# Block of two layers at one core: the first layer's projections, compressions and loads in another order

## What is computed

```python
def nsa_pool_mixer(x, w_in, cmp_pos, cmp_w1, cmp_b1, cmp_w2, pool_w, pool_scale, w_out):
    h = x @ w_in                       # columns: q 512 | six k/v of 128 | 24 gates | pool input u 512
    q = ...; kv = ...; gates = jax.nn.sigmoid(h[..., o2:o3]); u = h[..., o3:]
    k_cmp, v_cmp, k_slc, v_slc, k_win, v_win = kv
    kc = compress_blocks(k_cmp, cmp_pos[0], cmp_w1[0], cmp_b1[0], cmp_w2[0])   # gelu(blocks @ w1 + b1) @ w2
    vc = compress_blocks(v_cmp, cmp_pos[1], cmp_w1[1], cmp_b1[1], cmp_w2[1])
    ...                                # softmax over 15 compressed blocks -> o_c,
    ...                                # over the selected blocks -> o_s, over the window -> o_w
    o = gb[..., 0:1] * o_c + gb[..., 1:2] * o_s + gb[..., 2:3] * o_w
    o_pool = pool_mixer(u, pool_w, pool_scale)
    return jnp.concatenate([o_nsa, o_pool], axis=-1) @ w_out
```

## Time and profile before

| | |
|---|---|
| median of the runs | 1427.62 us |
| profiled execution | 1425.51 us, of it 1423.8 us span |
| PE (matmul) | 1313.5 us busy, 92% |
| PE weight loads | 1226.6 us, beside the matmuls |
| DVE | 832.3 us, 58% |
| ACT | 598.6 us, 42% |
| POOL | 176.6 us, 12% |
| chain that ended last | PE 77%, DVE 7%, ACT 6%, DMA 5%, POOL 3% |
| mean granted clock of PE | 0.953 |

### The profile page before, as it was taken

How to read it: one execution, slowest core, us unless ns; L and a number is a source line. 1 busy time by engine, 2 the same in 40 slices (tenths; PEclk the granted TensorE clock), 3 DMA queues, 4 the chain that set the end, 5 groups by cost and what they waited for, 6 DMA issues and landing times.

```text
span 1423.8 us, 20987 instructions
## 1 busy us (share of the span) xinstructions
PE 1313.5 (92%) x9100; PEld 1226.6 (86%) x9100; DVE 832.3 (58%) x970; ACT 598.6 (42%) x694; POOL 176.6 (12%) x136
## 2 busy tenths in 40 slices
PE   4898889999899879999898999889989899999996
PEld 4887789999799679999798999789989799999995
DVE  4425685555752785555769537764467665555554
ACT  3225544334464343433466237533743443333331
POOL 7030040000400040000221300031120300000002
PEclk9868999999999999999899999999999899999999
DMA  7350255555451545656689335963455436555550
GB/s 228 89 148 1 89 179 192 192 182 197 125 179 59 177 141 188 200 182 164 111 109 164 64 72 80 154 92 65 142 164 190 136 130 211 192 178 180 193 191 30
DMA packets 155021, 205.03 MB, mean 144 GB/s; under 512 B 9395, under 2 KB 137122, under 8 KB 154930
## 3 DMA queue, kind: packets, MB, share of 16 engines
q1 hardware_dynamic: 152706, 195.80, 49.6%
q0 software_dynamic: 2224, 7.90, 1.6%
HBM read 202.63 MB, written 1.05 MB: 143 GB/s over the span
## 4 chain that ended last, share of the span: by engine, by line
PE 77%; DVE 7%; ACT 6%; DMA 5%; POOL 3%; issue 2%; POOLq 0%; SPq 0%; DVEq 0%; ACTq 0%
PE PS L353 22%; PE PS L354 21%; PE PS L355 21%; DMA ring<-in_w_in 4%; DVE w_lo L965 2%; ACT w_hi L1514 2%; PE PS L810 2%; PE PS L822 1%; PE PS L818 1%; POOL lvl L1867 1%; POOL AR L1954 1%; ACT AR L1544 1%; DMA ring<-in_a_w_out 1%; PE PS L588 1%; DVE AR L1291 1%
## 5 line engine op out<-in xcount | busy, mean ns | idle before, releaser
L965 DVE TENSOR_TENSOR w_lo<-ring,w_hi 128x2048 fp32r<-128x2048 f32 x183 | 436.2, 2389 | 277.5 <-ACT w_hi L1514 267.4
L353 PE MATMUL PS<-x_hi,w_hi 128*128 128x256 f32 x1696 | 499.0, 294 | 37.4 <-DVE x_lo L1009 13.5
L354 PE MATMUL PS<-x_lo,w_hi 128*128 128x256 f32 x1696 | 490.6, 289 | 0.0
L355 PE MATMUL PS<-x_hi,w_lo 128*128 128x256 f32 x1696 | 489.9, 289 | 0.0
L1514 ACT ACTIVATE w_hi<-ring 128x2048 fp32r<-128x2048 f32 x183 | 349.2, 1911 | 314.7 <-PE PS L355 262.6
L353 PEld LDWEIGHTS PS<-x_hi,w_hi 128*128 128x128 f32 x1696 | 337.3, 199 | 45.1 <-DVE w_lo L965 24.9
L354 PEld LDWEIGHTS PS<-x_lo,w_hi 128*128 128x128 f32 x1696 | 337.0, 199 | 3.6 <-issue 2.0
L355 PEld LDWEIGHTS PS<-x_hi,w_lo 128*128 128x128 f32 x1696 | 336.3, 198 | 0.0
L1526 ACT ACTIVATE AR<-PS 128x512 f32<-128x512 f32 (+2 forms) x148 | 84.4, 584 | 332.8 <-PE PS L355 218.0
L353 PE MATMUL PS<-w_hi,o_hi 128*128 128x512 f32 x480 | 188.5, 393 | 4.2 <-DVE o_lo L1162 4.2
L354 PE MATMUL PS<-w_lo,o_hi 128*128 128x512 f32 x480 | 187.4, 390 | 0.0
(11 more groups left out here) (358 smaller groups left out, 1413.5 us busy)
## 6 DMA issues: line engine op xcount, KB each, us to landing
ring<-in_mlp_w SPq DMA_DIRECT2D x64, 1024.0 KB, 5.3
ring<-in_w_in SPq DMA_DIRECT2D x32, 1024.0 KB, 10.4
ring<-in_expert_w_gate SPq DMA_DIRECT2D x16, 1024.0 KB, 5.4
ring<-in_expert_w_up SPq DMA_DIRECT2D x16, 1024.0 KB, 5.4
ring<-in_expert_w_down SPq DMA_DIRECT2D x16, 1024.0 KB, 4.9
ring<-in_c_w_in SPq DMA_DIRECT2D x12, 1024.0 KB, 5.4
ring<-in_a_w_in SPq DMA_DIRECT2D x7, 1024.0 KB, 8.6
ring<-in_c_w_out SPq DMA_DIRECT2D x4, 1024.0 KB, 5.0
```

The lines of the kernel that those rows point to most:

```text
L353: mm(out, a_hi, b_hi, start=first, stop=False, skip_group_check=True)
L354: mm(out, a_hi, b_lo, start=False, stop=False, skip_group_check=True)
L355: return mm(out, a_lo, b_hi, start=False, stop=last, skip_group_check=True)
L965: v.tensor_tensor(w_lo[:, m % PARTS], ring[:, index[split[m]] % RING], w_hi[:, m % PARTS].bitcast(F32), ALU.subtract)\
```

## The change

- x is loaded in two halves, the first weight chunk too, and both are split half by half (ACT and DVE: x's two first pairs, first half of the weights, x's other pairs, second half). DVE no longer splits two whole chunks before x's low part; PE starts aq 0 when the first half is split.
- Chunks: aq 0, acmp, aq 1, au 0, au 1, cmp_w1, "ak" (both keys), "av" (both values). So acmp comes second, au before the keys, and keys and values fill a chunk each: ak is one `by_feature`, av one `by_token`, 48 matmuls of 256 columns each.
- ac1 is 16 matmuls of 60 columns with 128-column stationaries (both compressions side by side, loaded as two DMAs), and one stands after each of the 16 triples of au 1.
- The gates: 24 matmuls of 256 columns with the weights stationary, then two transposes of the result ("agT").
- Scores against compressed keys: 8 matmuls of 30 columns for 16 of 15. They stand before av, so that av's matmuls run while the compressed softmax is made.
- DVE's reciprocal covers 64 elements; the counts need fewer POOL instructions and come before POOL's level masks.
- The vector loads (16) follow three weight chunks; the small loads are in three groups between later chunks. The narrow weights are split in two parts.
- DVE's and ACT's splits of the first two output chunks stand elsewhere: on ACT both before the reading of av; on DVE one before the first maxima, one after the third.

The core of the diff (the loads and the split of the head; cut at "..."):

```diff
-        cols("aq", aw, 0, 2)
+        cols("aq", aw, 0, 1)
         cols("acmp", aw, 512, 1)
-        cols("akv", aw, 768, 2)
-        chunks.append(("cmp_w1", [((0, P), A["a_cmp_w1"][0].rearrange("v (k p) n -> p v k n", p=P), (2 * 16, 64))]))
+        cols("aq", aw, 256, 1, 1)
         cols("au", aw, 1304, 2)
+        chunks.append(("cmp_w1", [(v, A["a_cmp_w1"][0, v].rearrange("(k p) n -> p k n", p=P), (16, 64)) for v in range(2)]))
+        for name, c in (("ak", 768), ("av", 768 + P)):
+            chunks.append((name, [(a, aw[:, c + W * a:c + W * a + P].rearrange("(k p) n -> p k n", p=P), (KT, P)) for a in range(2)]))
...
+            by_feature(("aq", 0), lo=4, ready=[("xT", j) for j in range(4)], halves="first_lo")
             x_ready(-1)
-            by_feature(("aq", 1))
             by_feature(("acmp", 0))
...
+            by_feature(("aq", 1))
+            by_feature(("au", 0))
+            steps = triples(("au", 1), nxt())
             arrived(pe, "cmp_w1")
...
-            for v in range(2):
-                for k in range(16):
-                    ins = mm(ps[0:64, v * 32:v * 32 + 30], w[:, v, k, :], a_kb[:, v, k].rearrange("p g c -> p (g c)"), start=(k == 0), stop=(k == 15))
+            for k in range(16):
+                advance(steps, 1)
+                ins = mm(ps[:, 0:60], w[:, k, :], a_kb[:, :, k].rearrange("p v g c -> p v (g c)"), start=(k == 0), stop=(k == 15))
             close(ins, "ac1")
...
+            ins = with_x(ps[:, 0:T], "wga")
+            close(ins, "ag")
...
+            by_feature("ak")
...
+                    ins = mm(ps[:, o:o + 30], a_q[:, i, t * P:(t + 1) * P], a_kc.rearrange("p g c -> p (g c)"), start=True, stop=True)
+            close(ins, "asc")
+            by_token("av")
...
+            for h in range(2):
+                for j in (2 * h, 2 * h + 1):
+                    ve.wait_ge(S("x0_hi"), j + 1)
+                    ps = full(ve, ("xT", j))
+                    evacuated(v.tensor_tensor(flat(x_lo[:, 2 * j:2 * j + 2]), ps, flat(x_hi[:, 2 * j:2 * j + 2]).bitcast(F32), ALU.subtract), ("xT", j))
+                half = slice(h * PIECE // 2, (h + 1) * PIECE // 2)
+                ve.wait_ge(S("hi_split" if h else "first_hi"), 1)
+                ins = v.tensor_tensor(w_lo[:, 0, half], ring[:, 0, half], w_hi[:, 0, half].bitcast(F32), ALU.subtract)
...
-            v.reciprocal(a_rc, a_rc).then_inc(S("win_recip"), 1)
+            v.reciprocal(a_rc[:, :, 0:16], a_rc[:, :, 0:16]).then_inc(S("win_recip"), 1)
...
+                if n == 2:
+                    split_ahead(pieces_for["av"])
...
             for n, (name, parts) in enumerate(chunks):
-                if n == 2:
+                if n == RING:
                     load_vectors()
```

More of the change, by code:

```diff
@@ L355, in products, with by_feature @@
                 return mm(out, a_lo, b_hi, start=False, stop=last, skip_group_check=True)
-            def by_feature(chunk, a_hi=x_hi, a_lo=x_lo, lo=0, hi=8, ready=None, layer=None):
-                n = take(chunk)
+            def by_feature(chunk, a_hi=x_hi, a_lo=x_lo, lo=0, hi=8, ready=None, layer=None, halves=None):
+                if halves is not None:
+                    pe.wait_ge(S(halves), 1)
+                    n, reached[0] = part[chunk] % PARTS, part[chunk] + 1
+                else:
+                    n = take(chunk)
                 wh, wl = colview(w_hi, n), colview(w_lo, n)
@@ L366, in by_feature @@
                             read_out(pe, ready[k // 2])
+                        if m == 0 and k == 4 and halves is not None:
+                            take(chunk)
                         if m == 0 and k % 4 == 0 and layer is not None:
@@ L1560, in layer_norm, with queries @@
                     high_half(l, 1, 0)
-            for j in range(4):
-                ps = bank(("xT", j))
-                a(flat(x_hi[:, 2 * j:2 * j + 2]), ps, ACT.Copy).then_inc(S("x0_hi"), 1)
-            for j in range(2):
-                ps = bank(("aq", j)).rearrange("p (m t) -> p m t", m=2)
+            for h in range(2):
+                for j in (2 * h, 2 * h + 1):
+                    ps = full(act, ("xT", j))
+                    a(flat(x_hi[:, 2 * j:2 * j + 2]), ps, ACT.Copy).then_inc(S("x0_hi"), 1)
+                half = slice(h * PIECE // 2, (h + 1) * PIECE // 2)
+                if h:
+                    arrived(act, split[0])
+                else:
+                    act.wait_ge(S("first_weights"), 16)
+                a(w_hi[:, 0, half], ring[:, 0, half], ACT.Copy).then_inc(S("hi_split" if h else "first_hi"), 1)
+            pieces[0] = 1
+            def queries(j, ahead):
+                ps = bank(("aq", j), ahead).rearrange("p (m t) -> p m t", m=2)
                 for half in range(2):
@@ L1580, in _, with pool_input @@
-            act.wait_ge(S("small"), SMALL)
-            a(n_hi[:], narrow, ACT.Copy).then_inc(S("narrow_hi"), 1)
-            copy("ag", a_g, lambda ps: ps[:, 0:TT * 24].rearrange("p (t n) -> p t n", t=TT), func=ACT.Sigmoid)
-            ps = bank("ac1")
+            def pool_input(j):
+                ps = bank(("au", j), 1)
+                evacuated(a(a_u[0][:, 2 * j:2 * j + 2, 16:16 + T], ps.rearrange("p (a b) -> p a b", a=2), ACT.Copy), ("au", j))
+            queries(0, 2)
+            split_ahead(pieces_for[("acmp", 0)])
@@ L1590, in _ @@
             evacuated(ins, "ac1")
-            for j in range(2):
-                copy(("au", j), a_u[0][:, 2 * j:2 * j + 2, 16:16 + T], lambda ps: ps.rearrange("p (a b) -> p a b", a=2))
+            pool_input(1)
+            act.wait_ge(S("small"), SMALL)
+            a(n_hi[:, NARROW_PARTS[1]], narrow[:, NARROW_PARTS[1]], ACT.Copy).then_inc(S("narrow_hi"), 1)
+            ps = bank("ag")
+            evacuated(a(a_gT, ps[:, 0:T], ACT.Sigmoid), "ag")
+            ps = bank("ak", 1).rearrange("p (a t) -> p a t", a=2)
```

206 lines of the change are left out of this document (110 added, 96 removed).

## The result

The changed kernel took 1383.94 us (median of 4 runs, 1379.84 to 1389.86); the kernel before, beside it, 1429.19 (median of 4, one of them at 4461.28). The ratio is 0.9679, 95% interval 0.9646 to 0.9711: 3.2% faster. The prediction was 1380 us, range 1370 to 1394. The profiled execution spans 1381.1 us, before it 1423.8.

What follows compares the result with a forecast made beforehand. PE, 92% busy, bounds the kernel, with idle time and a low clock early. 59.6 + 2.2 + 9.9 = 71.7 us to the third unit, 49.0 earlier, less 1.7: 1425.51 becomes 1378.2, median put at 1380 us, range 1370 to 1394.

Steps and rivals of the forecast that it cites:

- Reference point: Third unit of scores, shared by both kernels: PE reaches it at 71.7 us in place of 120.74, 49.0 us earlier.
- Start: Loads and splits by halves: aq 0 begins at 10.2 us in place of 20.11; 11.8 if x's halves bring nothing.
- Work: PE's matmuls and transposes up to the third unit of scores: 59.6 us, plus 2.2 for first matmuls at the lower clock.
- Waits: PE's remaining waits up to the third unit of scores: 4.7 + 1.9 + 1 + 1.6 + 0.7 = 9.9 us.
- Covers: Chunks are split before PE wants them: acmp 1.3 us to spare, aq 1 4.6, cmp_w1 thinnest at 1.3; reciprocal hides.
- Given back: Loop: a whole DVE split behind the third maxima makes PE wait 1.7 us once (bounds 0 and 2.3); net 47.3 us.
- The clock: Up to the third unit, about 20 us of the gain is clock level; granted clock at 1.00 from about 15 us.
- Rival C: An input is late, through the DVE/POOL port lock or slow cmp_w1 and av loads: 6 to 14 us, 1390; chance 0.09.
- B: Clock falls again between the compressed scores and the loop, doubling about 9 us of work: 1389; chance 0.15.
- D: Clock fall and late input together, and the halves at the start bring nothing: 1403; chance 0.06.
- E: Slower: the clock level does not come back until the layer norm, costing 54 us: 1434; chance 0.02.
- Behind the norm: From the third unit to the end, distances stay those of before within 2 us; longer layers would show the prediction wrong.

Runs made afterwards that it cites:

- e2: Changed kernel with the start of before: x and the first weight chunk each in one load, two chunks split whole before x's low part; 1390.25 us.
- e3: Changed kernel with the gates as before, 48 matmuls moving 24 columns, at the new place behind au 1; 1388.07 us.
- e4: Changed kernel with the compression's 16 matmuls as one block behind au 1, not one after each triple; 1381.23 us.
- e10: Changed kernel with the 16 vector loads ahead of the third weight chunk, as before; 1377.45 us (1 run).
- e9: Changed kernel with DVE's full reciprocal of 1024 elements right behind x's low part; 1386.53 us.
- e7: Changed kernel with the loop's split of the second output chunk in four quarters behind the third to sixth maxima; 1383.97 us.
- e6: Kernel before with only the gates changed, to 24 matmuls of 256 columns at their old place, transposed back after au 1; 1422.44 us, ratio 0.9949.
- e8: Changed kernel with POOL's pooling sums held back until the compressed probabilities are written; 1380.86 us.
- e11: Changed kernel with x by column halves, compression in one block, av's bank read between ACT's splits, quartered loop split; aq 0's sum lacks a part; 1379.19 us.
- e12: The same four edits on the changed kernel as e11, with all terms of aq 0's sums; 1376.81 us, ratio to the kernel before 0.9619.

## Why the prediction was right, step by step

- **Reference point.** 71.7 us predicted for the third unit, 71.91 measured: 62.5 us of PE's busy time where I had 61.8, and 9.4 idle where I had 9.9. That closeness is partly luck: errors of both signs lie in it. Of the 48.8 us won, 8.7 lie ahead of aq 0, 33.7 between it and the scores and 6.4 behind them. The runs single out the halves (9.0, e2) and the gates' form (6.2, e3); the new order of the chunks was never undone alone, so what it gives is what the sum says, not a measured part.
- **Start.** 10.2 predicted; 11.38 in this profile, 10.10 to 10.64 in eight others. The step that failed in the one is the first half of the weights, taken to land at 7.6 and waited for until 9.01. e2 shows that the whole 9 us reach the norm.
- **Work.** The scores stood 44.8 us behind the start, predicted 44.3 (54.5 - 10.2). The compression was priced 3.2 with bounds to 6.2; it took 3.49 (e4). The compressed scores took 1.94, not 1.6, the values 3.81, not 3.3. Half of what a row shows at the lower level was a little too cheap each time.
- **Waits.** One of 1 us for the compressed keys was predicted, 0.35 came; ACT read av at 64.79, predicted 65, but PE waited only 0.33 us for it, not 1.6, because it came to the scores 1.7 us later than I had it. The transposed probabilities cost 0.73, predicted 0.7. These make up for the late start and the work.
- **Covers.** The thinnest, cmp_w1 with 1.3 us, held: no wait of PE from 13.80 to 55.8 us. e10 shows cover for the vector loads, e9 that the short reciprocal at its later place is worth 5.8 us in this order; I had only used that it hides.
- **Given back.** 1.7 predicted, 1.47 measured (e7). Net at the norm 47.3 predicted, 47.36 measured.
- **The clock.** That it holds from about 15 us on was right (15.85 in this profile). That 20 us of the gain are the level was not measured as one sum. The windows' clocks allow an estimate: each window's length times what its clock lacks to 1.00 is 20.6 us from 38.15 us on before and 1.8 from 11.38 to 36.92 after, so about 19, and that is an upper bound, since idle time is counted too. Of this e3 gives 3.8 us to the form of the gates, and e6 3.1 to the compression behind them. The reason was half right: behind a wait and wide matmuls it can fall (S1, e6), and with the narrow gates it falls without a wait (e3). The gates' new form was needed, not only the end of the wait.
- **Rival C.** The lock was on four instructions, 4.8 us of DVE, as its condition said; its price was wrong, since DVE's loss lay under PE's work (e8: 1.1 us up to the third unit). Rivals B, D and E did not come about.
- **Behind the norm** I wrote that the distances would be those of before within 2 us. In the profile they were 4.6 us longer (47.36 - 42.7), 3.6 of it S1. In e10, where S1 is short, the way from those second transposes (127.44) to the end is 1248.3 us, and 1247.7 before. By the prediction's own words, layers behind the norm that take longer are a sign of its being wrong, and in this profile they did. What failed is that it took one profile of before as fixed, not what it said of this change: the median, 4 us above the forecast, is within that scatter.

## What to carry to other kernels

Ask of every matmul group what it moves, also where PE never waits: here 48 narrow ones cost 6.2 us more than 24 wide ones, 2.4 of it because a narrow step is hardly shorter than a wide one and 2.4 in the work behind them. Give DVE's large splits no place inside a loop whose next step hangs on DVE; in pieces they were free. And judge a small edit by stages between marks that both kernels share, since a wait of 2 us cost 5 us of clock in one execution and nothing in the next.

## What the runs showed of the hardware that I had not expected

- The clock fell without any wait, during 48 matmuls of 24 columns (0.78, then 0.50, e3), and stayed at 1.00 through 32 records of 60 columns (e4), 16 of 30 (1.94 us, after) and even 64 of 30 (3.84 us, e6). What sets the first apart no run shows.
- At 1.00 a step was 0.11 us with 24, 30 or 60 columns moved and a stationary of 128 columns (e3, after, e4), 0.120 with 256, and 0.06 with 30 moved and a stationary of 64 (e6).
- Behind a wait of 2.0 us it fell in some executions and held in others (11 of 14 at S1, 5 of 14 at S2).
- Half of x by columns landed at 5.00 and 5.38 us, half by rows at 4.21 to 4.80, the whole at 5.86 to 6.18.
- In one PSUM bank the start flag of a second sum undid the first, unfinished one (e11, against e12).
